# A decoder block's last stage rebuilt: its weights loaded before the branch, split once and kept, and its projection taken one token tile at a time

## The chip, the cores and the metric

The kernel runs on one core of a Trainium2 chip. The metric is device time in microseconds (us) of one launch; lower is better.

## The reference

Two networks run one after the other on 256 tokens of width 1024, all in float32. The change touches the end of the second one:

```python
x = x + _hier_moe(_rmsnorm(x, norm_ffn_g[i]), ...)          # 32 experts, top 2
hp = _rmsnorm(x, norm_ple_g[i])
x = x + (p[i] @ w_ple[i]) * jax.nn.sigmoid(hp @ w_ple_gate[i])
return _rmsnorm(x, final_norm_g)
```

`w_ple` is 256 x 1024 and multiplies a per-token embedding p; `w_ple_gate` is 1024 x 1024. In the mixture of experts each expert has `w_gate_e`, `w_up_e` (1024 x 256) and `w_down_e` (256 x 1024).

## The kernel before

The program is written out by hand, engine by engine: the functions `tensor` (PE), `scalar` (ACT), `vector` (DVE), `gpsimd` and `sync` (SP) each issue their instructions in a fixed order and wait on semaphores. Nothing reorders them later.

**Weights.** SP issues every weight transfer on one queue, in the order of the list `units` (about 1 MB each). A unit goes to a slot of `ring` (7 slots of 8 KB per partition) or, in the mixture stage, of `ringx` (5 more). Before it issues a unit, SP waits until the unit that held that slot is used up. The stage of the experts is a stream: expert pair i (experts 2i and 2i+1) has four units of gate/up weights, each filled by two transfers (`w_gate_e`, `w_up_e`), and two units of down weights. Units 0 to 3 of the last pair, 15, sit in ring slots 0 to 3. The embedding weight follows in slot 6, which held a unit of pair 14, and the four units of the gate weight follow in slots 0 to 3: the first two wait for the first halves of `gate_up(15)`, the last two for its second halves (the semaphores `gate_up_used` and the bank's `full`).

**Splits.** Where precision asks for it, a float32 weight is split into a high part (an ACT copy to fp32r, `wh`) and the rest (a DVE subtraction, `wl`), in chunks of 128 x 1024: `split_hi` and `split_lo` with room for three chunks (`c % 3`), so a chunk waits until PE has used the one three before it. Each gate unit is two chunks. A product then takes three matmuls: high by high, high by low, low by high.

**Experts.** For each pair i PE does `gate_up(i)` (64-column weight tiles, 128 x 512), ACT the Silu into `fs`, DVE the product `fa`, PE two transposes (`act_T(i)`), ACT the copy `rt2` (`at2`, out of PSUM), PE `scatter(i - 1)` and `down(i)`, ACT and DVE the split halves `ysh` and `ysl` of the scaled result. `scatter(15)` closes the sum in banks 0 to 3, and DVE adds it to x (`add_x`).

**The branch.** If an expert has more than 64 tokens, a slow path computes the excess. Every engine but GpSimd reaches `general(...)`: it waits for the last `add_x`, loads a flag into a register and jumps over the path's body if the flag is 0, as it is here. On PE the body is some 450 rows long. SP issues the embedding and gate weights only behind its own branch.

**The end.** PE multiplies the embedding by `w_ple` (16 float32 matmuls) into banks 0 to 3. ACT squares x, DVE and ACT make the reciprocal root, both scale x into `xs` (`norm_T("np2")`), PE transposes it, ACT writes `hh` and DVE `hl`. `gemm_tok` then does the gate's projection: for each half of the columns, four chunks, both token tiles (96 matmuls). ACT takes the sigmoid, DVE multiplies and adds into x, and a last norm over both tiles (`norm_x`) goes out in two transfers of 512 KB.

Of the kernel before, what the change touches and what calls it, by code (L numbers as in the profile page):

```python
# [6 lines left out]
ALU = mybir.AluOpType  # L7
# [5 lines left out]
P = 128  # L13
# [78 lines left out]
def build(nc, A, out):  # L92
    with ExitStack() as ctx:
# [50 lines left out]
        def opened(*shapes):  # L144
# [41 lines left out]
        r1, S_, xg, ScT, ysh, ysl, xh, xl, smr, wsl, ringx = opened(  # L186
            ("S_", [P, 2, 2, 512], F32R), ("xg", [P, 2, 8, S], F32), ("ScT", [P, 4, S], F32R),
            ("ysh", [P, 2, DM], F32R), ("ysl", [P, 2, DM], F32R), ("xh", [P, 2, DM], F32R), ("xl", [P, 2, DM], F32R),
# [3 lines left out]
        r1, whp, wlp, sg, hhp, hlp = opened(*W2, ("sg", [P, 2, 1024], F32), *HH)  # L192
# [76 lines left out]
        c_gate = [split_of(cols_of(A["w_ple_gate_2"][0], n * 512, 512), 1024) for n in range(2)]  # L269
# [171 lines left out]
        flag = scr[:, 650:651].bitcast(I32)  # L441
# [6 lines left out]
        RV = {n: i + 1 for i, n in enumerate(("an0", "ckn", "fn0", "an1", "fn1", "mid", "nm2", "cq", "mln", "nf2", "np2", "fin"))}  # L448
        tnorm = {n: i for i, n in enumerate(("an0", "fn0", "an1", "fn1", "nm2", "nf2", "np2"))}
        SQ = {"an0": 4, "fn0": 8, "an1": 12, "fn1": 16, "mid": 17, "nm2": 21, "nf2": 25, "np2": 29, "fin": 30}  # L450
# [3 lines left out]
        def tensor(e):  # L454
# [585 lines left out]
            def scatter(i):  # L1040
                emptied(q, "ScT", i // 2)
                for n in range(2):
                    emptied(q, "dn", i, n)
                    for t in range(2):
                        b = claim(2 * t + n, "moe", t, n) if i == 0 else bank[2 * t + n]
                        for v in (ysh, ysl):
                            w = mm(b[:, :], ScT[:, i % 4, t * P:(t + 1) * P], v[:, i % 2, n * 512:(n + 1) * 512],
                                   i == 0 and v is ysh, i == 15 and v is ysl)
                        if i == 15:
                            w.then_inc(of(full, "moe", t, n), 1)  # L1050
                if i < 15:
                    ysc.inc(w, i)
# [30 lines left out]
            for n in range(2):  # L1083
                gemm_tok(("gate", n), "np2", c_gate[n], 512, hhp, hlp, whp, wlp, (4 + 2 * n, 5 + 2 * n))

        def scalar(e):
# [28 lines left out]
            def norm_T(name, ready, hh, c0=None, h2=None):  # L1115
# [14 lines left out]
                for i in range(4):  # L1130
                    if c0 is None and i % 2 == 0:
                        continue
                    b = filled(q, name, i)
                    for j in range(2):
                        k = 2 * i + j
                        w = act(hh[:, k, :], b[:, j * S:(j + 1) * S], ACT.Copy, scale=gain(name, k))
                        if c0 is not None:
# [285 lines left out]

            for part in range(2):
                gather(0, part)
            for i in range(16):
# [13 lines left out]
                for n in range(2):  # L1440
# [15 lines left out]
            act(xs[:, 0, :], x[:, 0, :], ACT.Square, accum_out=st[:, 0:1]).then_inc(s_sq, 1)  # L1456
            q.wait_ge(s_var, RV["fin"])
            act(st[:, 16:18], st[:, 8:10], ACT.Sqrt).then_inc(s_std, 1)

        def vector(e):  # L1460
# [48 lines left out]
            def rinv(name, n, width, o):  # L1509

                ts(st[:, 8:8 + n], st[:, 0:n], 1.0 / width, EPS, ALU.mult, ALU.add).then_inc(s_var, 1)
                q.wait_ge(s_std, RV[name])
                rcp(o, st[:, 16:16 + n]).then_inc(s_rstd, 1)
                q.wait_ge(s_rstd, RV[name])

            def norm_T(name, hh, hl=None, c0=None, h2=None, l2=None):
# [6 lines left out]
                if hl is not None:  # L1523
# [590 lines left out]

            select(0)
            for part in range(2):
                gather(0, part)
            for i in range(16):
# [13 lines left out]
                for n in range(2):  # L2132
# [4 lines left out]
                        ALU.subtract).then_inc(of(drained, "dn", i, n), 1)  # L2137
            add_x("moe")
# [3 lines left out]
            norm_T("np2", hhp, hlp, c_gate[0], whp, wlp)  # L2142
            for n in range(2):
                for c in range(4):
                    split_lo(min(c_gate[n] + c + 3, len(chunks)), whp, wlp)
                for t in range(2):
                    g_, o = sg[:, t, n * 512:(n + 1) * 512], x[:, t, n * 512:(n + 1) * 512]
                    emptied(q, ("gate", n), t)
# [4 lines left out]
            norm_x("fin", 1, xs, lambda: q.wait_ge(s_sgm, 4))  # L2153
# [16 lines left out]
        def sync(e):  # L2170
# [17 lines left out]
            for t in range(2):  # L2188
                q.wait_ge(s_xn, 3 + t)
                e.dma_start(od[:, t, :], xs[:, t, :]).then_inc(s_out, 16)  # L2190
            e.wait_ge(s_out, 32)
# [4 lines left out]
        wb = [ring[:, i, :] for i in range(3)]  # L2196
# [115 lines left out]
```

## Time and profile before

| | us |
|---|---|
| three runs | 1272.15, 1272.04, 1267.53; median 1272.04 |
| the profiled execution, its own time | 1272.39 |
| its span in the profile | 1270.6 |
| PE busy | 1126.4 (89%) |
| DVE busy | 625.7 (49%) |
| ACT busy | 498.8 (39%) |
| DMA, mean over the span | 177 GB/s |

The span runs from the first to the last recorded instruction; the execution's own time is 1.8 us more, outside the records. All times of day below are us from the span's start. The experts' stream fills the stretch from about 965 to 1216, and the part that the change rebuilds is the last 55 us.

### The profile page before, as it was taken

What the parts mean: (1) busy time and instruction counts of PE and PEld (TensorE: products, weight loads), DVE (VectorE), ACT (ScalarE), POOL (GpSimd) and SP (SyncE); (2) the same over time, 40 slices, a digit from 0 to 9 for tenths busy, and PEclk for the clock granted to TensorE, in tenths of its full rate; (3) what the DMA queues carried; (4) which work ended last, traced back from release to release, by engine and by line L of the source; (5) the groups of instructions that cost most, each with busy time, mean ns of one, the idle gap of its engine ahead of it and who ended that gap; (6) DMA issues with size and microseconds to landing.
All of it is one profiled execution on the core that took longest, in us unless ns stands there. A gap on an engine that the chain in (4) does not pass through costs nothing.

```text
span 1270.6 us, 15565 instructions
## 1 busy us (share of the span) xinstructions
PE 1126.4 (89%) x6207; PEld 883.4 (70%) x6207; DVE 625.7 (49%) x1222; ACT 498.8 (39%) x868; POOL 11.6 (1%) x10
## 2 busy tenths in 40 slices
PE   6777999899999899798999997978658999999866
PEld 5665768899988776687999986857545445554335
DVE  4677324666664554545676645656652112211135
ACT  5433212655553544335555535364231112121143
POOL 0000000000000000000000000000020000000000
PEclk9895657899999999779999998977878999999988
DMA  9520004456555443214565552320077999999940
GB/s 353 192 96 1 1 1 152 133 179 192 175 198 192 140 166 100 67 41 149 176 189 176 200 178 84 126 70 1 1 261 278 377 378 380 381 379 379 345 168 33
DMA packets 157502, 225.13 MB, mean 177 GB/s; under 512 B 9319, under 2 KB 124402, under 8 KB 157426
## 3 DMA queue, kind: packets, MB, share of 16 engines
q1 hardware_dynamic: 155168, 221.04, 51.3%
q10 hardware_dynamic: 2258, 3.05, 0.7%
q8 instruction: 51, 0.84, 0.3%
q14 instruction: 25, 0.20, 0.0%
HBM read 223.02 MB, written 1.05 MB: 176 GB/s over the span
## 4 chain that ended last, share of the span: by engine, by line
PE 80%; DVE 10%; ACT 4%; DMA 3%; issue 2%; SPq 1%; ACTq 1%; DVEq 0%
PE ps L472 73%; PE ps L476 6%; ACT xs L1091 1%; DVE wl L1467 1%; DMA pos<-in_positions_dram 1%; ACT wh L1094 1%; SPq L2186 1%; DMA ring<-in_w_up_e_dram 1%; DVE smb L1481 1%; DVE smb L1467 1%; DVE x L1467 1%; ACTq L1180 1%; DVE big L1733 0%; DVE xs L1467 0%; DVE sA L1477 0%
## 5 line engine op out<-in xcount | busy, mean ns | idle before, releaser
L1467 DVE TENSOR_TENSOR wl<-ring,wh 128x1024 fp32r<-128x1024 f32 (+2 forms) x220 | 267.8, 1220 | 242.5 <-ACT wh L1094 241.9
L1094 ACT ACTIVATE wh<-ring 128x1024 fp32r<-128x1024 f32 (+2 forms) x220 | 231.6, 1055 | 281.0 <-PE ps L472 275.1
L472 PE MATMUL ps<-hh,wh 128*128 128x256 f32 x768 | 219.9, 286 | 1.7 <-ACT sA L1094 0.9
L472 PE MATMUL ps<-hl,wh 128*128 128x256 f32 x768 | 218.2, 284 | 0.0
L472 PE MATMUL ps<-hh,wl 128*128 128x256 f32 x768 | 218.1, 284 | 0.0
L472 PEld LDWEIGHTS ps<-hh,wh 128*128 128x128 f32 x768 | 148.3, 193 | 3.2 <-issue 2.0
L472 PEld LDWEIGHTS ps<-hl,wh 128*128 128x128 f32 x768 | 148.2, 193 | 0.6 <-issue 0.5
L472 PEld LDWEIGHTS ps<-hh,wl 128*128 128x128 f32 x768 | 148.2, 193 | 0.0
L472 PE MATMUL ps<-wh,hh 128*128 128x512 f32 (+2 forms) x224 | 92.4, 412 | 6.0 <-DVE big L1485 2.7
L472 PE MATMUL ps<-ring,xg 128*64 128x512 f32 (+1 forms) x352 | 90.6, 565 | 1.9 <-DMA ring<-in_w_up_e_dram 1.9
L472 PE MATMUL ps<-wl,hh 128*128 128x512 f32 (+2 forms) x224 | 89.7, 400 | 0.0
L472 PE MATMUL ps<-wh,hl 128*128 128x512 f32 (+2 forms) x224 | 89.6, 400 | 0.0
L1091 ACT ACTIVATE pb<-smb,nbb 128x128 f32<-128x128 f32 x80 | 35.7, 447 | 97.6 <-DVE nbb L1472 97.6
L472 PEld LDWEIGHTS ps<-ring,xg 128*64 128x64 f32 (+1 forms) x352 | 31.5, 143 | 57.0 <-issue 52.9
L1477 DVE SCALAR_TENSOR_TENSOR ysl<-ps,wsl,ysh 128x512 fp32r<-128x512 f32 x32 | 24.0, 751 | 91.9 <-ACT ysh L1091 91.9
L476 PE MATMUL ps<-cst,xs 128*128 128x128 f32 x160 | 33.0, 392 | 39.0 <-ACT xs L1091 30.4
L476 PEld LDWEIGHTS ps<-cst,xs 128*128 128x128 f32 x160 | 30.1, 211 | 41.9 <-ACT xs L1091 32.6
L472 PE MATMUL ps<-ringx,xg 128*64 128x512 f32 x192 | 57.4, 593 | 1.0 <-DMA ringx<-in_w_up_e_dram 1.0
L1467 DVE TENSOR_TENSOR fa<-ps,fs 128x256 f32<-128x256 f32 x16 | 6.8, 425 | 101.0 <-ACT fs L1091 101.0
L472 PEld LDWEIGHTS ps<-wh,hh 128*128 128x128 f32 x224 | 44.2, 197 | 17.2 <-issue 7.9
L472 PE MATMUL ps<-wl,ffh 128*128 128x512 f32 x176 | 54.3, 389 | 0.0
L472 PE MATMUL ps<-wh,ffh 128*128 128x512 f32 x176 | 54.2, 390 | 0.0
(237 smaller groups left out, 1718.8 us busy)
## 6 DMA issues: line engine op xcount, KB each, us to landing
ring<-in_w_up_dram SPq DMA_DIRECT2D x88, 512.0 KB, 4.8
ring<-in_w_down_dram SPq DMA_DIRECT2D x22, 1024.0 KB, 4.9
ring<-in_w_gate_e_dram SPq DMA_DIRECT2D x40, 512.0 KB, 10.3
ring<-in_w_up_e_dram SPq DMA_DIRECT2D x40, 512.0 KB, 9.2
ringx<-in_w_down_e_dram SPq DMA_DIRECT2D x16, 1024.0 KB, 9.6
ring<-in_w_down_e_dram SPq DMA_DIRECT2D x16, 1024.0 KB, 10.7
ring<-in_w_in_odd_dram SPq DMA_DIRECT2D x12, 1024.0 KB, 5.1
ringx<-in_w_gate_e_dram SPq DMA_DIRECT2D x24, 512.0 KB, 8.3
```

Of the source, the lines that this page charges most:

```text
L472: return e.matmul(o, l, r, start=start, stop=stop)
L476: return e.transpose(o, i, cst[0:n, C_ID:C_ID + n])
L1091: return e.activation(o, i, f, **kw)
L1094: return e.activation(o, i, ACT.Copy)
L1180: e.dma_start(dst, src).then_inc(s_c, 16)
L1467: return e.tensor_tensor(o, a, b, op)
L1477: return e.scalar_tensor_tensor(out=o, in0=a, scalar=s, in1=b, op0=o1, op1=o2)
L1481: return e.tensor_tensor_reduce(out=o, in0=a, in1=b, scale=1.0, scalar=init, op0=o1, op1=o2, accum_out=ac)
L2186: e.dma_start(view(slot[k]), src).then_inc(loaded[k], 16)
```

## The change

- SP issues the embedding and gate weights before its branch, right behind the last expert's; the slow path now uses `ringx` for its weights, and its flag moves to a tile that nothing overwrites.
- All eight split chunks of the gate weight have room of their own, `wg` (64 KB per partition, over tiles of the expert stage). The first three are split in the expert loop, at the end of iteration i = 14; the other five after the norm.
- The gate's projection takes token tile 0 over all eight chunks, then tile 1. The sigmoid, product, sum, final norm and stores of tile 0 come before those of tile 1; squares are on ACT alone, in halves, and stores are four of 256 KB.
- `scatter` goes through the banks by token tile, and ACT has `warm()` (a square root of a constant) before the branch and before the last squares.

```diff
@@ tiles @@
-        r1, S_, xg, ScT, ysh, ysl, xh, xl, smr, wsl, ringx = opened(
+        r1, S_, xh, xl, xg, ScT, ysh, ysl, smr, wsl, ringx = opened(
...
-        r1, whp, wlp, sg, hhp, hlp = opened(*W2, ("sg", [P, 2, 1024], F32), *HH)
+        r1, wg, hhp, hlp, sg = opened(("wg", [P, 8, 2, 1024], F32R), *HH, ("sg", [P, 2, 1024], F32))
@@ tensor: scatter @@
-                for n in range(2):
+                for t, n in ((0, 0), (0, 1), (1, 0), (1, 1)):
                     emptied(q, "dn", i, n)
-                    for t in range(2):
@@ tensor, end @@
             norm_T("np2")
-            for n in range(2):
-                gemm_tok(("gate", n), "np2", c_gate[n], 512, hhp, hlp, whp, wlp, (4 + 2 * n, 5 + 2 * n))
+            for t in range(2):
+                tk = slice(t * P, (t + 1) * P)
+                for c in range(8):
+                    n = c // 4
+                    q.wait_ge(w_split, c_gate + c + 1)
+                    emptied(q, "np2", c % 4)
+                    for k in (2 * (c % 4), 2 * (c % 4) + 1):
+                        b = claim(4 + 2 * t + n, "gate", t, n) if k == 0 else bank[4 + 2 * t + n]
+                        wh_, wl_ = (wg[:, c, i, (k % 2) * 512:(k % 2 + 1) * 512] for i in range(2))
+                        mm(b[:, :], hhp[:, k, tk], wh_, k == 0, False)
+                        mm(b[:, :], hhp[:, k, tk], wl_, False, False)
+                        w = mm(b[:, :], hlp[:, k, tk], wh_, False, k == 7)
@@ scalar @@
+            def gate_hi(upto):
+                while hi[0] < c_gate + upto:
+                    c = hi[0]
+                    u, half, n, _ = chunks[c]
+                    copy(wg[:, c - c_gate, 0, :], unit_in(q, u)[:, half * n:(half + 1) * n]).then_inc(w_hi, 1)
+                    hi[0] += 1
...
                     act(ysh[:, i % 2, n * 512:(n + 1) * 512], b[:, :], ACT.Copy, scale=wsl[:, i:i + 1]).then_inc(s_yh, 1)
+                if i == 14:
+                    filled(q, "wsl", 7)
+                    gate_hi(3)
+            warm()
             general(e, "ACT")
...
-            norm_T("np2", added("moe"), hhp, c_gate[0], whp)
-            for n in range(2):
-                for c in range(4):
-                    split_hi(min(c_gate[n] + c + 3, len(chunks)), whp)
-                for t in range(2):
-                    b = filled(q, ("gate", n), t)
-                    act(sg[:, t, n * 512:(n + 1) * 512], b[:, :], ACT.Sigmoid).then_inc(of(drained, ("gate", n), t), 1)
-            q.wait_ge(s_sgm, 3)
-            act(xs[:, 0, :], x[:, 0, :], ACT.Square, accum_out=st[:, 0:1]).then_inc(s_sq, 1)
-            q.wait_ge(s_var, RV["fin"])
-            act(st[:, 16:18], st[:, 8:10], ACT.Sqrt).then_inc(s_std, 1)
+            norm_T("np2", added("moe"), hhp, hl_too=True)
+            gate_hi(8)
+            for t in range(2):
+                for n in range(2):
+                    b = filled(q, "gate", t, n)
+                    act(sg[:, t, n * 512:(n + 1) * 512], b[:, :], ACT.Sigmoid).then_inc(of(drained, "gate", t, n), 1)
+                if t:
+                    warm()
+                for n in range(2):
+                    c = slice(n * 512, (n + 1) * 512)
+                    q.wait_ge(s_sgm, 2 * t + n + 1)
+                    act(xs[:, t, c], x[:, t, c], ACT.Square, accum_out=st[:, 2 * n + t:2 * n + t + 1]).then_inc(s_sq, 1)
+                q.wait_ge(s_var, RV[f"fin{t}"])
+                act(st[:, 16 + t:17 + t], st[:, 8 + t:9 + t], ACT.Sqrt).then_inc(s_std, 1)
@@ vector: gate_lo as gate_hi, subtracting into wg[:, c - c_gate, 1, :] @@
+                if i == 14:
+                    gate_lo(3)
             add_x("moe")
             general(e, "DVE")
...
+            norm_T("np2", hhp, hlp)
+            gate_lo(8)
...
+                q.wait_ge(s_sq, SQ[f"fin{t}"])
+                own.inc(tt(st[:, t:t + 1], st[:, t:t + 1], st[:, 2 + t:3 + t], ALU.add))
+                rinv(f"fin{t}", 1, DM, st[:, 24 + t:25 + t], t)
+                for n in range(2):
+                    c = slice(n * 512, (n + 1) * 512)
+                    stt(xs[:, t, c], x[:, t, c], st[:, 24 + t:25 + t], gfin[:, 1, c], ALU.mult, ALU.mult).then_inc(s_xn, 1)
@@ sync @@
             for u, (_, parts) in enumerate(units):
-                if u == u_ple:
-                    general(e, "SP")
...
+            general(e, "SP")
...
-            for t in range(2):
-                q.wait_ge(s_xn, 3 + t)
-                e.dma_start(od[:, t, :], xs[:, t, :]).then_inc(s_out, 16)
+            for i in range(4):
+                t, c = i // 2, slice((i % 2) * 512, (i % 2 + 1) * 512)
+                q.wait_ge(s_xn, 3 + i)
+                e.dma_start(od[:, t, c], xs[:, t, c]).then_inc(s_out, 16)
```

How this moves instructions stands in the built programs. On SP, the issues around the branch (TENSOR_LOAD begins it). Before:

```order
L2186 DMA ring<-in_w_down_e_2_dram 128x2x1024 [waits full7]
L2186 DMA ring<-in_w_down_e_2_dram 128x2x1024
L2202 TENSOR_LOAD smb_14 [waits drained3,flag_ready]
...
L2186 DMA ring<-in_w_ple_2_dram 128x2x1024 [waits gate_up_used]
L2186 DMA ring<-in_w_ple_gate_2_dram 128x4x512 [waits gate_up_used] x3
L2186 DMA ring<-in_w_ple_gate_2_dram 128x4x512 [waits full6]
```

With the change:

```order
L2225 DMA ring<-in_w_down_e_2_dram 128x2x1024 [waits full7]
L2225 DMA ring<-in_w_down_e_2_dram 128x2x1024
L2225 DMA ring<-in_w_ple_2_dram 128x2x1024 [waits gate_up_used]
L2225 DMA ring<-in_w_ple_gate_2_dram 128x4x512 [waits gate_up_used] x3
L2225 DMA ring<-in_w_ple_gate_2_dram 128x4x512 [waits full6]
L2243 TENSOR_LOAD st [waits drained3,flag_ready]
```

The five transfers now stand ahead of the branch, with the same waits.

On ACT, from the last `ysh` of iteration 14 to the first of iteration 15 (`fs<-ps6` is the Silu of `gate_up(15)`; `loaded0` and `loaded1` count the landings in ring slots 0 and 1). Before:

```order
L1091 ACTIVATE ysh_14<-ps4,wsl_14 128x512 [waits y_scattered,full4,drained6]
L1091 ACTIVATE ysh_14<-ps5,wsl_14 128x512 [waits full5]
L1091 ACTIVATE fs<-ps6 128x256 [waits full6]
L1094 ACTIVATE rt2<-ps7 128x256 [waits full7]
L1091 ACTIVATE ysh_14<-ps4,wsl_14 128x512 [waits y_scattered,full4]
```

With the change:

```order
L1103 ACTIVATE ysh_14<-ps5,wsl_14 128x512 [waits full5]
L1106 ACTIVATE wg_15<-ring 128x1024 [waits loaded0]
L1106 ACTIVATE wg_15<-ring 128x1024
L1106 ACTIVATE wg_15<-ring 128x1024 [waits loaded1]
L1103 ACTIVATE fs<-ps6 128x256 [waits full6]
L1106 ACTIVATE rt2<-ps7 128x256 [waits full7]
```

Three copies of gate chunks, with waits for the first two gate units, stand ahead of the Silu; on DVE three subtractions stand ahead of `fa` in the same way.

## Rows read from the trace of the kernel before

**Rows 1.** The chain of waits, from 1191 us on: start, length, what it was.
```profile
1191.86 9.34 DMA ring<-in_w_up_e_dram
...
1201.25 3.66 PE ps L472 x14
...
1205.42 0.43 DVE fa L1467
...
1214.18 1.89 DVE x L1467 x3
...
1217.44 5.61 DMA ring<-in_w_ple_dram
...
1223.09 9.41 PE ps L472 x16
...
1236.51 23.01 PE ps L472 x93
```
**Rows 2.** Timeline of SP: its last weight issues (start, length, engine, line, operation).
```profile
1193.22 2.63 SPq L2186 DMA_DIRECT2D ring<-in_w_down_e_dram  x2
1217.44 0.37 SPq L2186 DMA_DIRECT2D ring<-in_w_ple_dram  x1
1217.86 4.15 SPq L2186 DMA_DIRECT2D ring<-in_w_ple_gate_dram  x4
```
**Rows 3.** Stretches: length, busy us by engine, granted PE clock, DMA share, GB/s.
```profile
532.00:558.00 26.00, 26.00 (x104) 21.74 (x105) 9.22 (x37) 8.71 (x33) 0.00 (x0) 0.50 0.00 1
...
1203.00:1206.00 3.00, 2.00 (x9) 0.53 (x6) 0.42 (x1) 0.38 (x1) 0.00 (x0) 1.00 0.30 123
...
1217.50:1223.10 5.60, 0.01 (x1) 0.01 (x1) 1.38 (x5) 5.27 (x12) 0.00 (x0) 0.50 0.83 287
1223.10:1227.50 4.40, 4.40 (x5) 1.83 (x6) 0.36 (x1) 1.06 (x1) 0.00 (x0) 0.50 1.05 393
1227.70:1232.50 4.80, 4.80 (x14) 2.12 (x13) 0.67 (x1) 0.00 (x0) 0.00 (x0) 1.00 1.03 378
1238.10:1241.00 2.90, 2.90 (x8) 2.26 (x7) 1.32 (x2) 0.16 (x1) 0.00 (x0) 0.50 0.00 0
```
**Rows 4.** Timeline of PE: its last matmul before the branch.
```profile
1214.22 0.40 PE L472 MATMUL ps<-ysl,ScT 128*128 128x512 f32 x1
```
**Rows 5.** The branch's line (L2202) by engine: durations in ns, first and last start.
```profile
L2202 ACTq COMPARE_BRANCH  x1: 50/50/50, 1216.9 to 1216.9; - x1
L2202 PEldq COMPARE_BRANCH  x1: 3862/3862/3862, 1217.1 to 1217.1; - x1
```
**Rows 6.** Timeline of ACT and DVE behind the branch.
```profile
1217.39 0.63 ACT L1091 ACTIVATE xs<-x 128x512 f32<-128x512 f32 x1 [4.88 <-issue]
...
1219.96 1.28 ACT L1091 ACT_TABLE_LOAD   x1
1221.26 0.20 ACT L1091 ACTIVATE st<-st 128x2 f32<-128x2 f32 x1
1221.70 1.33 ACT L1091 ACTIVATE xs<-x,st 128x512 f32<-128x512 f32 x2 [0.23 <-DVE st L1493]
1226.05 1.06 ACT L1094 ACTIVATE wh<-ring 128x1024 fp32r<-128x1024 f32 x1 [3.02 <-DMA ring<-in_w_ple_gate_dram]
1227.14 1.23 DVE L1467 TENSOR_TENSOR wl<-ring,wh 128x1024 fp32r<-128x1024 f32 x1 [4.56 <-ACT wh L1094]
```
**Rows 7.** Timeline of the end.
```profile
1259.80 0.39 PE L472 MATMUL ps<-wh,hl 128*128 128x512 f32 x1
1261.51 0.68 DVE L1467 TENSOR_TENSOR sg<-sg,ps 128x512 f32<-128x512 f32 x1
1262.23 0.69 DVE L1467 TENSOR_TENSOR x<-x,sg 128x512 f32<-128x512 f32 x1
1264.29 0.17 DVE L1473 TENSOR_SCALAR st<-st 128x2 f32<-128x2 f32 x1
1264.93 2.48 DVE L1477 SCALAR_TENSOR_TENSOR xs<-x,st,gfin 128x1024 f32<-128x1024 f32 x2
```

More of the change, by code:

```diff
@@ L268, in build @@
                              A["w_ple_2"][0].rearrange("(k p) n -> p k n", p=P)))
-        c_gate = [split_of(cols_of(A["w_ple_gate_2"][0], n * 512, 512), 1024) for n in range(2)]
+        c_gate = [split_of(cols_of(A["w_ple_gate_2"][0], n * 512, 512), 1024) for n in range(2)][0]
         place, in_slot, landed = {}, [None] * (NU + NX), [0] * (NU + NX)
@@ L440, in build @@
         tot = scr[:, 616:648]
-        flag = scr[:, 650:651].bitcast(I32)
+        flag = st[:, 63:64].bitcast(I32)
         def slots_of(i, t):
@@ L1041, in scatter @@
                 emptied(q, "ScT", i // 2)
-                for n in range(2):
+                for t, n in ((0, 0), (0, 1), (1, 0), (1, 1)):
                     emptied(q, "dn", i, n)
-                    for t in range(2):
[L1045 to L1050, printed above, removed]
+                    b = claim(2 * t + n, "moe", t, n) if i == 0 else bank[2 * t + n]
+                    for v in (ysh, ysl):
+                        w = mm(b[:, :], ScT[:, i % 4, t * P:(t + 1) * P], v[:, i % 2, n * 512:(n + 1) * 512],
+                               i == 0 and v is ysh, i == 15 and v is ysl)
+                    if i == 15:
+                        w.then_inc(of(full, "moe", t, n), 1)
                 if i < 15:
@@ L1082, in tensor @@
             norm_T("np2")
-            for n in range(2):
-                gemm_tok(("gate", n), "np2", c_gate[n], 512, hhp, hlp, whp, wlp, (4 + 2 * n, 5 + 2 * n))
+            for t in range(2):
[10 more added lines that the diff above has]
+                        w = mm(b[:, :], hlp[:, k, tk], wh_, False, k == 7)
+                    if k == 7:
+                        w.then_inc(of(full, "gate", t, n), 1)
         def scalar(e):
@@ L1113, in warm, with norm_T @@
                 act(st[:, 62:63], cst[:, C_ONE:C_ONE + 1], ACT.Sqrt)
-            def norm_T(name, ready, hh, c0=None, h2=None):
+            def norm_T(name, ready, hh, c0=None, h2=None, hl_too=False):
                 for t in range(2):
@@ L1130, in norm_T @@
                 for i in range(4):
-                    if c0 is None and i % 2 == 0:
+                    if c0 is None and not hl_too and i % 2 == 0:
                         continue
@@ L1136, in norm_T @@
                         w = act(hh[:, k, :], b[:, j * S:(j + 1) * S], ACT.Copy, scale=gain(name, k))
-                        if c0 is not None:
+                        if c0 is not None or hl_too:
                             w.then_inc(s_hh, 1)
@@ L1522, in norm_T @@
                     ts(xs[:, 1, c], x[:, 1, c], st[:, 25:26], None, ALU.mult).then_inc(s_xsd, 1)
-                if hl is not None:
+                if c0 is not None:
                     split_lo(c0 + 1, h2, l2)
@@ L2113, in gather, with gate_lo @@
                 cp(xg[:, g % 2, 2 * m:2 * m + 2, :].rearrange("p k c -> p (k c)"), b[:, :]).then_inc(of(drained, "xg", g, m), 1)
+            def gate_lo(upto):
+                while lo[0] < c_gate + upto:
+                    c = lo[0]
+                    u, half, n, _ = chunks[c]
+                    q.wait_ge(w_hi, c + 1)
+                    tt(wg[:, c - c_gate, 1, :], slot[place[u][0]][:, half * n:(half + 1) * n],
+                       wg[:, c - c_gate, 0, :].bitcast(F32), ALU.subtract).then_inc(w_split, 1)
+                    lo[0] += 1
             select(0)
@@ L2137, in vector @@
                         ALU.subtract).then_inc(of(drained, "dn", i, n), 1)
+                if i == 14:
+                    gate_lo(3)
             add_x("moe")
             general(e, "DVE")
[L2142 to L2145, printed above, removed]
-                for t in range(2):
+            norm_T("np2", hhp, hlp)
+            gate_lo(8)
+            for t in range(2):
+                for n in range(2):
                     g_, o = sg[:, t, n * 512:(n + 1) * 512], x[:, t, n * 512:(n + 1) * 512]
-                    emptied(q, ("gate", n), t)
+                    emptied(q, "gate", t, n)
                     b = filled(q, "ple", t, n)
```

21 lines of the change are left out of this document (10 added, 11 removed).

## The prediction

> **What bounds the kernel now.** I read the chain of waits first, for the path that sets the end. Through the experts it is the weight stream: PE waits for the last expert's weights until 1201.25 [rows 1]. From there it is one dependent chain: the second half of `gate_up(15)`, ended 1204.9; Silu and `fa` at 1205.42; PE to the last matmul of `scatter(15)`, ended 1214.6 [rows 4]; `add_x`, ended 1216.07 [rows 1]; the branch; the landing of the embedding weight, from 1217.44 to 1223.05; sixteen embedding matmuls, 9.41 us; transposes and `hh`/`hl`; the gate's 96 matmuls from 1236.51 to 1260.2 [rows 1, 7]; and a tail of 10.4 us to the end of the span at 1270.6.
>
> The timeline of SP shows that its queue stands idle from 1195.85 (1193.22 + 2.63) to 1217.44 [rows 2]: the change wants this hole. The stretches show why the hole in the queue is no hole in the transfers: the engines move at full rate until 1203 and only drain from 1203 to 1206 [rows 3]. They show the clock of TensorE too: at 1.00 (2.4 GHz) while the experts run, and at 0.50 (1.2 GHz) from 1217.5, some 3 us after PE fell idle, until 1227.5, that is for 4.4 us after it had work again.
>
> **The change part by part.** *The early split.* On ACT three copies of gate chunks now stand ahead of the Silu of pair 15, and the third waits for the second gate unit. When does that land? The stream from 1203 to 1206 moved 3 x 123 GB/s = 0.37 MB; at 378 to 393 GB/s [rows 3] that is 1.0 us, so evenly spread it would have ended at 1204.0, and its slowest engine ended near 1206. Behind it come the embedding unit and two gate units, 3.15 MB or 8.1 us. None is issued too late to follow on: the first two gate units wait only for the first halves of `gate_up(15)`, over before PE's wait for the last expert's weights, which ends at 1201.25 [rows 1]. So the landing lies between 1212.1 (even) and 1214.1 (the slowest engine's); a unit has landed only when its slowest engine has, so I take 1213.6, near the upper end. The first two copies are over by then. Then 1.06 us for the third copy and 1.23 for its subtraction [rows 6], with gaps: `fa` starts at 1216.0 where it started at 1205.42. **+10.6 us.** Queued behind the waiting instructions are the Silu, `rt2` and both `ysh` on ACT, `fa`, both `ysl` and `add_x` on DVE; and PE, which cannot transpose before `fa`, nor run `scatter(14)`, which stands behind the transposes.
>
> *The clock in the rest of pair 15.* PE now idles from 1204.9 to about 1216.5, longer than the 8.5 us ahead of 1223.09 [rows 1], after which the clock stayed low for 4.4 us [rows 3]. Taken the same, 4.4 us at half speed lose **2.2 us**. Bounds: 1.4 us from the shortest low stretch shown, 2.9 us; 5.7 us if the clock stays low as in the 26 us from 532 [rows 3]. `add_x` then ends at 1216.07 + 12.8 = 1228.9.
>
> *The wait for the embedding weight* is gone: it has landed by about 1208. What is late next? ACT restarted 1.32 us after `add_x` (1217.39), but PE's jump over the slow path took 3.86 us, from 1217.1 to 1221.0, against 0.05 on ACT [rows 5, 6]. It was hidden under the transfer; now it is bare. PE can start 4.9 us after `add_x`, not 7.0: **-2.1 us**. That is all that the early load brings at this place. PE will start at 1233.8 after 6.4 us of idling, so I keep the sixteen matmuls at 9.41 us, with 4.4 us of low clock; with no low stretch they would take 7.2 (bound: -2.2). Running sum +10.7 where the transposes start: 1243.2.
>
> *The norm beside it.* The square root of `warm()` makes one table load more, ahead of the squares: 1.28 us [rows 6]. ACT's path from its restart to the scaled x was 5.6 us (1217.39 to 1223.03), now 6.9: from 1230.2 to 1237.1, 6.1 us before PE is free. Nothing, as long as PE's restart stays late; without that cover the norm would set the start of the transposes from 1237.1 on.
>
> *The splits kept, and the gate by token tile.* The matmuls are the same 96. A chunk now lasts PE six matmuls (1.36 us at 23.01/93 less the low stretch, about 0.227 each) instead of twelve; ACT makes one in 1.06 and DVE in 1.23, and three are ready, so PE does not wait. Bank 5 is no longer needed at the second matmul group, a wait of 0.2 us: **-0.2**. The low stretch of 2.9 us at 1238.1 [rows 3] I leave as it is; without it, -1.4. `scatter` by token tile: `add_x` takes the banks in the new order anyway, and its 1.89 us for three [rows 1] are DVE's own: 0.
>
> *The tail*, from the end of the last matmul: 10.4 us before. Now: sigmoid 0.60; then on ACT table load and root of `warm()`, 1.5, beside product and sum on DVE, 1.4 (0.68 + 0.69 [rows 7]); two squares, 1.4 with the read of the sum; four small steps, 0.7 with gaps 0.9; two halves of the product with the gain, 1.25 (half of 2.48 [rows 7]); and the store, 3.2 us before for 512 KB, between 2.5 and 3.2 for 256 KB, taken as 2.85. Sum 8.5, with 0.1 of gaps 8.6: **-1.8 us**. Tile 0's part lies beside tile 1's matmuls, 10.9 us. The table load here took 1.28 us and the root started 0.02 us behind it (1219.96, 1221.26 [rows 6]).
> The Trainium skill (ScalarE: Activation LUTs, What ACT_TABLE_LOAD costs) adds a drain and puts each switch at about 2.66 us. By that rule the tail would be 1.4 us longer and the estimated sum +10.1; the row shows no drain, and it decides.
>
> **Sum:** 10.6 + 2.2 - 2.1 - 0.2 - 1.8 = **+8.7 us**. The profiled execution took 1272.39, 0.35 above the median of 1272.04; against the median this gives **1280.7 us**. About 0.5% (6.4 us) is what a measurement of this kernel can tell from no change, so the bounds are 1265.7 and 1278.4.
>
> **The rivals.**
> *A, the loads come in time.* If the gate units landed before the Silu is due at 1204.93, the terms +10.6 and +2.2 go, and -4.1 is left: 1267.9. For it: SP is free from 1195.85, and the order of two transfers on sixteen engines is not shown by any row. Against: 3.15 MB more would have to move by 1204.9 on engines that were full until 1203. It decides if the third copy starts before about 1206. This is the case on the other side; it stays a small gain because of PE's jump, and only with a shorter store and a warm clock as well would it pass 1265.7.
> *B, PE's jump is short.* Its 3.86 us coincided with SP's issue of five transfers, which will be absent. If it was these that held it up, PE restarts with ACT, 1.3 us after `add_x`: -3.6, and after a shorter idle about -1.0 for the clock: 1276.1. Against: ACT, DVE and SP jumped at the same moment in under 0.1 us, and the transfers moved 287 GB/s on average from 1217.5 to 1223.1 [rows 3], 1.6 MB, so at full rate they ran only from about 1219.
> The Trainium skill (Runtime: NRT & Kernel Launch, Instruction fetch mechanics) says that a taken branch whose target lies outside the window of prefetched pages must fetch it by DMA before the engine goes on. By this the 3.86 us belong to PE's long slow path and stay; it is why B gets no more than it does, and the trace agrees as far as one jump can.
> *C, the clock stays low* from the restart at 1216.5 through the embedding matmuls. For it: two long gaps close together, and 26 us of low clock with PE busy from 532 on [rows 3]. Against: after the one gap shown here PE had the clock back in 4.4 us. Price: 5.7 + 0.7 for the last scatter instead of 2.2, and 13.6 for 9.4 us: +8.4, 1289.
>
> **How the numbers follow.** The forecast has 0.71, A 0.12, B 0.12, C 0.05. The forecast's own range: downward the landing 1.5, the clock 0.8 + 2.2 + 1.4, the store 0.35; upward the landing 0.5, the store 0.35, a longer low clock 1.5, a drain 1.4. Not all fall together: 1276 to 1284. The range that holds 8 in 10 takes in B and the edges on both sides, and leaves out A and C: 1269 to 1286. Of the forecast's 0.71, 0.58 lie above 1278.4. Slower: 0.58 + 0.05 = 0.63. Within 0.5%: 0.13 + 0.12 (B) + 0.08 (A) = 0.33. Faster: 0.04, the rest of A.
>
> **What the profile would show.** If I am right: the third copy into `wg` starts near 1213.6 behind a wait for `ring<-in_w_ple_gate_dram`; `fa` of pair 15 at about 1216; PE idle for over 10 us before it and the clock at 0.50 behind it; PE's COMPARE_BRANCH again near 3.9 us, and embedding matmuls that wait for nothing but it, from about 1234; the gate's matmuls without waits for `wg`; 8 to 9 us from the last matmul to the end. I am wrong if the Silu starts before 1210, if PE's jump takes under 1 us, or if the clock is back within 1 us of the restart.

## The result and the profile after

| | us |
|---|---|
| with the change, four runs | 1279.93, 1280.49, 1280.09, 1281.36; median 1280.29 |
| before, four runs (the three shown and 1267.32) | median 1269.78 |
| ratio | 1.008, 95% interval 1.0055 to 1.0104 |
| the profiled execution: own time, span | 1279.93, 1278.1 |

The change makes the kernel 0.8% slower. The two kernels' profiled executions lie 7.5 us apart (1279.93 for 1272.39), the medians 10.5: two of the kernel before's four runs are near 1267.4 and two near 1272.1, while all four of the change are near 1280 (the end of the section on the prediction says what hangs on that).

The chain of waits of the changed kernel, from 1188 us on (start, length, what it was), answers to [rows 1]:

```profile
1188.43 9.41 PE ps L473 x40
...
1197.86 15.95 DMA ring<-in_w_ple_gate_dram
...
1213.83 1.07 ACT wg L1106
...
1214.91 0.30 DVE wg L1493
...
1216.06 0.43 DVE fa L1493
1216.48 0.04 issue
1216.53 0.69 PE ps L477 x2
...
1226.47 1.89 DVE x L1493 x3
1228.36 4.98 issue
1233.34 9.03 PE ps L473 x16
...
1246.38 23.66 PE ps L473 x96
```

The chain no longer leads through the experts' last weights: for 16 us it is the transfer of the gate weight, then the third early copy and its subtraction, then `fa`. Behind the last sum stand 4.98 us in which PE waits for nothing that the profile shows. 3.82 of them are PE's jump; the rest is mostly the load of the flag ahead of it. The branch's line and SP's timeline, answering to [rows 5] and [rows 2]:

```profile
L2243 ACTq COMPARE_BRANCH  x1: 50/50/50, 1229.2 to 1229.2; - x1
...
L2243 PEldq COMPARE_BRANCH  x1: 3822/3822/3822, 1229.4 to 1229.4; - x1
```
```profile
1195.19 0.66 SPq L2225 DMA_DIRECT2D ring<-in_w_ple_dram  x1
1197.33 10.04 SPq L2225 DMA_DIRECT2D ring<-in_w_ple_gate_dram  x4
```

The timeline of ACT shows the wait and, at the end, the tail:

```profile
1213.83 1.06 ACT L1106 ACTIVATE wg<-ring 128x1024 fp32r<-128x1024 f32 x1 [0.71 <-DMA ring<-in_w_ple_gate_dram]
1214.79 0.37 ACT L1103 ACTIVATE fs<-ps 128x256 f32<-128x256 f32 x1
...
1270.06 0.60 ACT L1103 ACTIVATE sg<-ps 128x512 f32<-128x512 f32 x1 [4.65 <-PE ps L473]
1270.68 1.28 ACT L1103 ACT_TABLE_LOAD   x1
1271.97 0.20 ACT L1103 ACTIVATE st<-cst 128x1 f32<-128x1 f32 x1
```

And the stretches (columns as in [rows 3]: length, busy us by engine, granted clock of PE, DMA share, GB/s):

```profile
1203.00:1206.00 3.00, 1.39 (x6) 0.21 (x2) 0.00 (x0) 0.00 (x0) 0.00 (x0) 1.00 1.02 403
1207.00:1216.50 9.50, 0.00 (x0) 0.00 (x0) 3.92 (x4) 3.33 (x4) 0.00 (x0) 0.50 1.01 373
1216.50:1220.10 3.60, 3.57 (x10) 2.80 (x10) 0.00 (x0) 0.38 (x1) 0.00 (x0) 0.50 0.12 46
1220.30:1223.90 3.60, 3.60 (x17) 1.05 (x16) 0.73 (x1) 0.69 (x1) 0.00 (x0) 1.00 0.00 0
```

From 1203 to 1206 the engines moved 403 GB/s instead of 123: the stream does not drain, it goes on. PE idles at half clock (1.2 GHz) and has 3.6 us of work before the clock is back at 2.4 GHz.

**Where the time went.** All kernels below are compared in one stretch, from the end of `gate_up(15)` (1204.90 before, 1204.39 with the change) to the end of the span. What lies ahead of it is the same code in all of them but for the order of the banks in `scatter`, yet the end of `gate_up(15)` varies by up to 11 us from one profiled execution to the next (last section). Each number is the start of the named instruction in the timeline less the end of `gate_up(15)`; the last two are ends.

| kernel | fa | end of last sum | embedding product | transposes | gate | last matmul | end of span |
|---|---|---|---|---|---|---|---|
| before | 0.52 | 11.16 | 18.19 | 27.44 | 31.61 | 55.29 | 65.70 |
| the change | 11.67 | 23.96 | 28.95 | 37.82 | 41.99 | 65.64 | 73.71 |
| e1_split_late | 0.52 | 11.16 | 16.23 | 26.07 | 30.25 | 52.25 | 60.33 |
| e2_loads_only | 0.52 | 11.18 | 15.92 | 24.50 | 28.67 | 52.32 | 62.76 |
| e3_short_body | 0.52 | 11.17 | 12.74 | 21.18 | 26.08 | 49.67 | 57.78 |
| e4_one_chunk | 8.99 | 21.02 | 25.79 | 34.62 | 38.79 | 62.51 | 70.65 |
| e5_wait_inside | 0.53 | 11.17 | 15.38 | 24.32 | 28.49 | 52.12 | 60.26 |
| e6_transposes_first | 0.52 | 11.17 | 19.77 | 16.04 | 26.23 | 48.60 | 56.75 |
| e7_filler | 11.68 | 22.32 | 26.85 | 36.81 | 40.98 | 63.03 | 71.16 |
| e8_all | 0.52 | 11.16 | 19.45 | 15.93 | 25.92 | 48.29 | 55.81 |
| e9_before_short | 0.53 | 11.17 | 18.62 | 27.61 | 31.78 | 55.48 | 65.87 |
| e10_late_pair | 0.52 | 11.16 | 12.92 | 22.86 | 27.04 | 49.06 | 57.14 |
| e11_product_around | 0.52 | 11.17 | 12.91 | 17.86 | 24.67 | 46.73 | 54.32 |

The runs' times agree with this table once that variation is taken out. Each run has a granted clock, its mean over the span, and the runs of one kernel fall into groups by it. The group with the lowest clock (0.898 to 0.904), less the same group of the kernel before in the same session (0.899 to 0.900):

| kernel | runs in the group, median | against the kernel before | in the stretch |
|---|---|---|---|
| e1_split_late | 6, 1267.4 | -4.7 | -5.4 |
| e2_loads_only | 8, 1269.4 | -2.6 | -2.9 |
| e3_short_body | 9, 1264.8 | -7.2 | -7.9 |
| e4_one_chunk | 8, 1277.0 | +4.9 | +4.95 |
| e5_wait_inside | 7, 1266.5 | -5.5 | -5.4 |
| e6_transposes_first | 3, 1263.6 | -8.5 | -8.95 |
| e7_filler | 3, 1277.3 | +5.3 | +5.5 |
| e8_all | 7, 1262.5 | -9.6 | -9.9 |
| e9_before_short | 6, 1272.0 | +0.2 | +0.2 |
| e11_product_around | 3, 1261.3 | -10.5 | -11.4 |

### The profile page after: what moved, and what is told of

Read it like the earlier page. It is cut to its first block, busy times and chain, and to the rows that moved or that the text cites. A ratio compares the mean times of both kernels' runs of the same rounds, so it can differ in the third digit from the quotient of the medians.

```text
span 1278.1 us, 15581 instructions
## 1 busy us (share of the span) xinstructions
PE 1127.0 (88%) x6207; PEld 884.0 (69%) x6207; DVE 625.7 (49%) x1226; ACT 506.0 (40%) x881; POOL 11.6 (1%) x10
## 4 chain that ended last, share of the span: by engine, by line
PE 79%; DVE 10%; ACT 4%; DMA 3%; issue 2%; SPq 1%; ACTq 1%; DVEq 0%
PE ps L473 73%; PE ps L477 6%; ACT xs L1103 2%; DVE wl L1493 1%; DMA ring<-in_w_ple_gate_dram 1%; DMA pos<-in_positions_dram 1%; ACT wh L1106 1%; DVE smb L1507 1%; DVE smb L1493 1%; SPq L2225 1%; DMA ringx<-in_w_up_e_dram 1%; ACTq L1192 1%; DVE x L1493 1%; DVE xs L1493 0%; DVE big L1759 0%
## 5 line engine op out<-in xcount | busy, mean ns | idle before, releaser
L1493 DVE TENSOR_TENSOR wl<-ring,wh 128x1024 fp32r<-128x1024 f32 (+2 forms) x212 | 258.3, 1220 | 231.2 <-ACT wh L1106 230.5
L1106 ACT ACTIVATE wh<-ring 128x1024 fp32r<-128x1024 f32 (+2 forms) x212 | 223.3, 1055 | 269.2 <-PE ps L473 266.2
L473 PE MATMUL ps<-wh,hh 128*128 128x512 f32 (+2 forms) x192 | 78.9, 411 | 3.8 <-DVE big L1511 2.7
L473 PE MATMUL ps<-wl,hh 128*128 128x512 f32 (+2 forms) x192 | 76.3, 397 | 0.0
L473 PE MATMUL ps<-wh,hl 128*128 128x512 f32 (+2 forms) x192 | 75.9, 395 | 0.0
L473 PE MATMUL ps<-wh,ffl 128*128 128x512 f32 x176 | 54.2, 389 | 0.0
```

What stands on the lines that cost most here:

```text
L473: return e.matmul(o, l, r, start=start, stop=stop)
L1106: return e.activation(o, i, ACT.Copy)
L1493: return e.tensor_tensor(o, a, b, op)
```

## The experiments

The theory going in: the wait for the second gate unit and the clock it lets fall cost 12.8 us, and PE's jump eats most of what the early load could give back.

**e1_split_late: the early split undone.**

```diff
-                if i == 14:
-                    filled(q, "wsl", 7)
-                    gate_hi(3)
...
-            norm_T("np2", added("moe"), hhp, hl_too=True)
+            norm_T("np2", added("moe"), hhp, hl_too=True, mid=lambda: gate_hi(3))   # behind the scaling of xs
```
(and the same on DVE with `gate_lo`)

> The changed kernel with one part undone: no gate chunk is split inside the expert loop; the first three are split on ACT and DVE behind the norm's scaling, while PE does the embedding product. Theory (the third copy waits for the second gate unit and holds up the Silu of pair 15, which also lets PE's clock fall): both terms go, 10.6 + 2.2, so about 12.5 us under the changed kernel and 4.1 us under the kernel before; the Silu of pair 15 within 0.5 us of its place in the kernel before, the embedding product about 2 us earlier than there because it starts when PE's jump ends. Rival (the loss comes from the transfers themselves or from the new tail, and the split's place is innocent): the time stays within 2 us of the changed kernel.

Measured: 1264.15 us median against 1271.45 for the kernel before on the same chip, ratio 0.9957 (0.9934 to 0.998); some 16 us under the change, of which 3 are the higher clock of half of its runs (its six at 0.900 to 0.902 have a median of 1267.4, 12.9 under the change). In the stretch 13.4 us under the change, 5.4 under the kernel before. The Silu of pair 15 starts 0.04 us behind `gate_up(15)`, as before. So nearly all the loss hangs on where three copies stand, and not on the transfers or the new tail. The 1.3 us beyond the forecast 4.1 are no gain of the edit alone: the gate's matmuls took 22.0 us and not 23.65, since the low stretch in them was absent, while the product took 10.01 for 9.41; the tail gave 0.5 more than forecast.

**e2_loads_only: the early loads alone, in the kernel before.**

```diff
-                if u == u_ple:
-                    general(e, "SP")
...
+            general(e, "SP")
             od = out[0].rearrange("(t p) d -> p t d", p=P)
...
-        wb = [ring[:, i, :] for i in range(3)]
+        wb = [ringx[:, i, :] for i in range(3)]
```

> The kernel before with one part of the change alone: SP issues the embedding and gate weights ahead of its branch. Theory (PE's jump over the slow path takes 3.9 us and stood hidden under the transfer): 2.1 us faster than the kernel before, the embedding product starts at the end of PE's COMPARE_BRANCH, 4.9 us after the last sum. Rival 1 (the jump was held up by SP's issues at the same moment): PE restarts about 1.3 us after the sum and the gain is 5.7 us or more. Rival 2 (the extra transfers behind the experts' delay the last expert weights): no gain, and PE waits past 1201.3 for the last expert's weights.

Measured: 1269.0 median, ratio 0.9991 (0.9968 to 1.0014); by all its runs it cannot be told from the kernel before. The stretch shows what happened, 2.9 us less, and the runs of like clock show 2.6. In its chain of waits there is a hole of 4.7 us where the transfer of 5.61 us stood:

```profile
1213.84 1.89 DVE x L1467 x3
1215.73 4.73 issue
1220.46 8.74 PE ps L472 x16
```

The product starts 2.27 us earlier (15.92 for 18.19) and is 0.67 shorter (8.74 for 9.41). Rival 1 is out; so is rival 2, for the last expert's weights come no later: the wait for them ends at 1200.89 here, 1201.25 before.

**e3_short_body: PE has little to jump over.**

```diff
-            for n in range(32):
+            for n in range(1):
```
(in the four bodies of the slow path, on top of e1_split_late; `g_dve` is waited for accordingly)

> The first experiment's kernel with the slow path cut to expert 0 (it leaves out the excess of the other 31 experts; that path is jumped over here). Theory (the target of PE's jump lies far behind the body, and its instructions have to be fetched): PE's COMPARE_BRANCH falls from 3.9 us to under 0.2, PE restarts about 1.3 us after the sum, and the kernel gains 2 to 4 us over the first experiment, less than 3.6 where the norm on ACT then sets the start of the transposes. Rival (a fixed price of a jump on PE, or the flag's load): the jump keeps 3.8 us and the time is the first experiment's.

The branch's line on PE, in e1_split_late and then here:

```profile
L2242 PEldq COMPARE_BRANCH  x1: 3885/3885/3885, 1208.5 to 1208.5; - x1
```
```profile
L2242 PEldq COMPARE_BRANCH  x1: 365/365/365, 1217.6 to 1217.6; - x1
```

The price of the jump goes with the length of what is jumped over: 3.89 us over 32 experts' rows, 0.37 over one's (these two lengths alone were tried). The trace shows what it is. DMA queue 8 carries packets of 16 KB of the kind "instruction". In the eleven kernels with the long body such a packet lies inside PE's jump, and the jump ends 1.3 to 1.4 us after the packet has landed: 1209.99 to 1210.95 in e1_split_late, whose jump ends at 1212.34. In the two with the short body none does; the next begins 0.75 us behind the jump. So PE waits for a fetch of instructions.

The restart comes 3.5 us earlier, the end of the stretch only 2.55. The product was 1.4 us shorter than in e1_split_late (8.61 for 10.01); against that the transposes to the gate took 0.7 more (4.90 for 4.18), because ACT still had the three copies ahead of `hh`, and the gate's matmuls 1.6 more, their low stretch being back. The medians show none of it: 1264.68 against 1264.15, ratios 0.9958 and 0.9957. But only one of the ten runs here has a clock above 0.902, against six of twelve in e1_split_late; the groups of lowest clock lie 2.6 us apart (1264.8 and 1267.4), as the stretch does. The expected gain of 2 to 4 us held.

**e4_one_chunk: a shorter wait.**

```diff
-                    gate_hi(3)
+                    gate_hi(1)
...
-                    gate_lo(3)
+                    gate_lo(1)
```

> The changed kernel with one chunk split early in place of three, so that the Silu of pair 15 waits for the first gate unit alone. Theory (the stall ends at a landing): the copy starts near 1211.1 as in the changed kernel, the Silu near 1212.1, DVE's product fa near 1213.4 instead of 1216.06; about 2.6 us faster than the changed kernel, still some 5.5 us slower than the kernel before. Rival (the stall is the time of the copies and subtractions on ACT and DVE): two of three pairs of 1.0 and 1.2 us go, and the product starts 2.2 us after the ysl of pair 14, near 1198, before its data is there, so that the whole loss vanishes.

```profile
1211.61 1.06 ACT L1106 ACTIVATE wg<-ring 128x1024 fp32r<-128x1024 f32 x1 [16.39 <-DMA ring<-in_w_ple_gate_dram]
1212.58 0.37 ACT L1103 ACTIVATE fs<-ps 128x256 f32<-128x256 f32 x1
```

Measured: 1276.73 median, ratio 1.0049 (1.003 to 1.0067). `fa` starts 2.7 us sooner than with three chunks, by the distance between the two landings, and 4.95 of the 8.0 us of loss stay. One copy of 1.06 us holds up the Silu by 7.7. The rival (the work of splitting) is out.

**e7_filler: the idle without the clock's fall.**

```diff
                 b = take("aT", i)
+                if i == 15:
+                    for _ in range(12):
+                        mm(b[:, :], cst[:, C_ID:C_ID + P], cst[:, C_MA:C_MA + 512], True, True)
                 emptied(q, "gu", i)
```

> The changed kernel with twelve float32 matmuls of constants on PE, some 10 us, into the bank that the transposes of pair 15 overwrite, issued while PE waits for fa; nothing of the result depends on them. Theory (the idle of 12 us costs the clock besides the wait itself): fa stays near 11.7 us behind the end of gate_up(15), the clock stays at 1.00 through scatter(14), its matmuls are 0.23 us apart and not 0.43, and from fa to the last sum it takes 10.6 us as in the kernel before instead of 12.3, so about 1.7 us less in the stretch to the end. The clock after PE's jump can come out either way, worth up to 2 us. Rival (scatter(14) and down(15) are slow for another reason, such as transfers or port traffic): 12.3 us and 0.43 us stay.

Its stretches around `fa`, which starts at 1207.32 there:

```profile
1196.00:1207.00 11.00, 10.13 (x24) 4.18 (x22) 3.19 (x3) 3.34 (x4) 0.00 (x0) 1.00 1.04 387
1207.40:1211.00 3.60, 3.21 (x16) 2.01 (x18) 0.33 (x1) 0.38 (x1) 0.00 (x0) 1.00 0.21 79
```

With PE kept busy through the wait its clock stays at 2.4 GHz, and from `fa` to the last sum it takes 10.64 us, exactly as in the kernel before, against 12.29 with the change. The clock's share of the loss is 1.65 us. The whole stretch is 2.55 us shorter than with the change: besides the 1.65, PE's jump is 0.46 shorter (3.36 for 3.82) and the gate's matmuls, without a low stretch here too, 1.6 (22.05 for 23.65), while the product takes 1.1 longer (10.12 for 9.03). Median 1272.9, ratio 1.0043 (1.0013 to 1.0072).

**e9_before_short: the jump in the kernel before.** The edit of e3_short_body, on the kernel before.

> The kernel before with the slow path cut to expert 0 (it leaves out the excess of the other 31; the path is jumped over). Theory (in the kernel before PE's jump is hidden under the embedding weight's transfer): COMPARE_BRANCH falls from 3.9 us to some 0.4, the embedding product still starts at the landing, 18.2 us behind gate_up(15), and the time stays within 0.3%. Rival (the jump cost the kernel before something too): the product starts earlier and the stretch to the end falls by over 1 us.

Measured: 1271.54 against 1271.27, ratio 1.0 (0.9978 to 1.0022), with COMPARE_BRANCH at 0.36 us and the product at 18.62. The jump cost the kernel before nothing; it was under the transfer.

**e5_wait_inside: jump earlier.**

```diff
             b, n = use["moe", 1, 1]
-            e.wait_ge(drained[b], n + 1)
             with e.If(e.value_load(flag[0:1, :], min_val=0, max_val=1) > 0):
+                e.wait_ge(drained[b], n + 1)
```
(on top of e1_split_late)

> The first experiment's kernel; the wait for the last sum stands inside the slow path instead of ahead of its test, so that all engines jump as soon as they reach it. Theory (PE's jump of some 3.7 us is bare): PE jumps right behind scatter(15), 1.4 us earlier, and the embedding product starts 14.8 us behind gate_up(15) instead of 16.2; 1.4 us faster than the first experiment, 59 us from gate_up(15) to the end. Rival (the norm on ACT, with its added table load, sets the transposes): the embedding product starts earlier but the transposes do not, and nothing is gained.

Measured: 1266.24, ratio 0.9958 (0.9934 to 0.9982), no better than e1_split_late; the stretch 0.07 us shorter. The transposes start 1.75 us earlier, but the gate's matmuls take 1.6 more (23.63 for 22.00), their low stretch being back. The product starts 0.85 us earlier, not 1.4. The jump begins 2.8 us earlier and takes 5.7 us:

```profile
L2241 PEldq COMPARE_BRANCH  x1: 5745/5745/5745, 1214.5 to 1214.5; - x1
```
```profile
1214.50:1216.00 1.50, 0.83 (x4) 0.34 (x2) 1.50 (x3) 1.49 (x2) 0.00 (x0) 1.00 1.04 384
1216.00:1218.00 2.00, 0.00 (x0) 0.00 (x0) 0.32 (x1) 2.00 (x8) 0.00 (x0) 0.93 0.73 268
```

The second fence has the stretches in which it lies: the gate weights were still streaming. The instruction packet begins 3.3 us behind the start of the jump (1217.82 for 1214.54), against 1.0 to 1.5 in the kernels that jump behind the sum, and the jump ends 1.4 us after it, as there. So it is the start of the fetch that is late. This was a miss, and gave the next question.

**e10_late_pair: no stream beside the jump.**

```diff
+                if u >= u_ple + 3:
+                    emptied(q, "moe", 1, 1)
                 for view, src in parts:
                     e.dma_start(view(slot[k]), src).then_inc(loaded[k], 16)
```
(on SP, on top of e5_wait_inside)

> The kernel with the wait inside the slow path (PE's jump there took 5.7 us and not 3.8), with the last two gate units issued only behind the last sum, so that no weight transfer runs while PE's jump begins. Theory (the jump has to fetch instructions over the same DMA engines, and the weight stream, at full share until 1216 there, delayed that fetch): PE's COMPARE_BRANCH falls from 5.7 to some 3.7 us, the embedding product starts 13.2 to 13.7 us behind gate_up(15) instead of 15.4. Rival (the jump waits for something of PE's own, such as the matmuls still running when it is reached): 5.7 us stay.

```profile
L2243 PEldq COMPARE_BRANCH  x1: 3367/3367/3367, 1215.6 to 1215.6; - x1
```
```profile
1215.60:1217.00 1.40, 0.81 (x4) 0.35 (x2) 1.40 (x3) 1.39 (x2) 0.00 (x0) 1.00 0.04 12
```

With 12 GB/s beside it instead of 384 the same jump takes 3.37 us, although PE's own matmuls still run when it begins, as in e5_wait_inside. The product starts 12.92 us behind `gate_up(15)`, even before the 13.2 expected. The instruction packet begins 1.0 us behind the start of the jump. The rival is out. This kernel was run once (1265.22 us); its profile is what is read.

**e6_transposes_first** moves `norm_T("np2")` on PE ahead of the embedding product (on top of e5_wait_inside) and splits all eight chunks behind `hh` and `hl`.

> The kernel with the wait inside, and on PE the transposes of the scaled x ahead of the embedding product, so that ACT and DVE make hh, hl and the first split chunks under it; all eight chunks are split behind hh and hl. Theory: the 4.2 us from the transposes to the first gate matmul leave the path; the transposes start when the norm is ready, which the table load behind the jump sets, near 17 us behind gate_up(15), the gate at 28 to 29, and the stretch ends near 57. Rival (the splits of the first chunks now come too late, since hl ends first): PE waits for w_split between the product and the gate, and less than 2 us is gained.

Measured: 1258.69, ratio 0.9911 (0.9873 to 0.9949). `hh`, `hl` and the first splits now lie under the product, and the gate starts 2.3 us earlier than in e5_wait_inside. The transposes started at 16.0, not 17, and the gate at 26.2, not 28 to 29.

**e8_all** moves `warm()` from ahead of the branch to behind it, and squares the first half ahead of the last sigmoid.

> The previous kernel with warm() behind the branch instead of ahead of it, which takes the extra table load off the norm's path, and with the square of the first half ahead of the last sigmoid. Theory: the transposes start when PE's jump ends, near 14.8 us behind gate_up(15) instead of 17, the gate near 26, and the tail is 0.6 us shorter than 8.1; 54 to 55 us from gate_up(15) to the end against 65.7 in the kernel before, about 0.9% faster than it. Rival (PE's clock, low after the idle of the jump, takes the gain back in the transposes and the embedding product): above 57 us.

Measured: 1262.25, ratio 0.9939 (0.9912 to 0.9966). The tail is 7.52 us instead of 8.15, as expected. The gain at the transposes did not come (15.93 against 16.04). Two things end late and nearly together, and I had reckoned with neither. PE's jump takes 5.7 us (6.0 in e6_transposes_first) and ends at 1215.08. The norm is later still, and it is what the transposes wait for:

```profile
1214.31 0.16 DVE L1491 TENSOR_TENSOR st<-st 128x2 f32<-128x2 f32 x1 [3.16 <-issue]
```
```profile
1215.92 3.39 PE L477 MATMUL ps<-cst,xs 128*128 128x128 f32 x14 [5.76 <-ACT xs L1103]
```

ACT's last square was done at 1212.07, yet DVE's first step of the norm began at 1214.31, 3.1 us behind DVE's own COMPARE_BRANCH of 0.07 us. The same hole of 2.8 to 3.2 us stands there in all five kernels in which the squares are done early (e5, e6, e8, e10, e11). So DVE seems to pay for its jump as well, behind the branch's row and not in it; a run that shortens DVE's path alone was not made, so this is not shown. 55.8 us for the stretch against 54 to 55 expected.

**e11_product_around** puts the two findings together.

```diff
             for t in range(2):
+                if t:
+                    norm_T("np2")
                 for n in range(2):
                     b = claim(2 * t + n, "ple", t, n)
```
(on top of e8_all, with the edit of e10_late_pair)

> The kernel with all changes so far, with the last two gate units issued behind the last sum as in e10_late_pair, and with the embedding product of token tile 0 ahead of the transposes and that of tile 1 behind them, since PE is then free before the norm is ready. Theory: the product starts near 13.4 us behind gate_up(15), the transposes at 17 to 18, the gate at 23 to 24 instead of 25.9; 53 to 54 us to the end instead of 55.8, about 1% under the kernel before. Rival (the transfers issued behind the sum land too late for the fifth chunk, or PE's low clock stretches the first half of the product): the gate starts at 25 us or later, or PE waits inside it.

Measured: 1258.38 us median against 1271.27, ratio 0.9908 (0.9884 to 0.9932): 0.9% faster than the kernel before and 1.7% under the change (1258.38 to 1280.29, medians of two sessions). It has the shortest stretch, 54.32 us against 65.70 and 73.71. The gate started at 24.67, not 23 to 24; the timeline of PE shows it waiting 0.65 us for the first split at the end:

```profile
1212.69 5.11 PE L473 MATMUL ps<-ring,ppT 128*128 128x512 f32 x8 [2.73 <-issue]
...
1220.20 3.60 PE L473 MATMUL ps<-ring,ppT 128*128 128x512 f32 x8
1224.45 0.73 PE L473 MATMUL ps<-wg,hh 128*128 128x512 f32 x2 [0.65 <-DVE wg L1492]
```

By time e6_transposes_first is as good; the stretch tells them apart (56.75 and 54.32), the runs do not.

## Why the prediction was right

| step | forecast | measured in the stretch |
|---|---|---|
| `fa` waits for the second gate unit | +10.6 | +11.15 (11.67 for 0.52) |
| low clock behind the wait | +2.2 | +1.65 (12.29 for 10.64 from `fa` to the end of the last sum) |
| wait for the embedding weight gone, PE's jump bare | -2.1 | -2.04 (4.99 for 7.03) |
| embedding product | 0 | -0.38 (9.03 us for 9.41) |
| start of the transposes to the gate | 0 | 0.00 (4.17 both) |
| gate's 96 matmuls | -0.2 | -0.03 |
| tail | -1.8 | -2.34 (8.07 for 10.41) |
| sum | +8.7 | +8.0 |

The steps are differences of the table's rows, the lengths of the product from the two chains of waits.

- **The landing.** Forecast at 1213.6 between 1212.1 and 1214.1; the copy started at 1213.83. Behind the end of `gate_up(15)`, which came 0.5 us earlier than before, that is 9.44 us and not 8.7, just past the upper bound of 9.2. The end of the slowest engine was the better of the two guesses; which engine ended last was not read. e4_one_chunk shows that the landing sets the stall.
- **The clock.** The mechanism is shown by e7_filler. 2.2 was too high: PE worked at the low clock for only 3.6 us, until 1220.1, not 4.4.
- **The jump.** That the early load would give only 2.1 us was the least obvious step. e2_loads_only bears it out, and e3_short_body with its instruction packets shows the cause. The Trainium skill (Runtime: NRT & Kernel Launch, Instruction fetch mechanics) says that a taken branch out of the prefetched pages stalls for a fetch by DMA; 3.89 us against 0.37 agree with it. Rival B was half right: transfers do lengthen the jump, but those of the kernel before came too late to do so (3.86 us with them, 3.82 without, the instruction packet 1.0 us behind the start of the jump in both). The prediction's "ACT, DVE and SP jumped at the same moment in under 0.1 us" reads the branch's rows alone: DVE's next instruction there starts 3.19 us behind its branch, some 0.4 us after the last square. With the change the squares end later (1233.51, and DVE goes on at 1233.54), so this cost nothing here.
- **The tail** was mis-sized by 0.5 us. From the last matmul to the start of the last two products with the gain it took 4.2 us (1270.04 to 1274.25), forecast 4.4 to 4.5; the rest is their length and the store of 256 KB.
- **The table load** is not dearer than its row: 1.28 us, and the root 0.01 us behind it. The Trainium skill's drain (ScalarE: Activation LUTs, What ACT_TABLE_LOAD costs) does not show here: the load follows the sigmoid by 0.02 us. The 1.4 us for a drain in the forecast's own range upward has thus no row of this kernel.
- **Rivals A and C** did not come. In A the third copy would have started before 1206. In C the clock would have stayed low; it was back after 3.6 us. (C's 13.6 us for the product at low clock should be 14.4, twice the 7.2 that the prediction has at full clock; its price is 0.8 too small, and nothing else rests on it.)

That the median came within 0.4 us of the forecast is partly luck. The sum was 0.7 us too high in the stretch. The median of the kernel before moved from 1272.04 to 1269.78 with one run more, and 8.7 on top of that would have been 1278.5. It helped that no run of the change fell into a group of higher clock: all four had 0.896 to 0.897. The forecast was reckoned from the kernel before's level near 1272, which in its later runs goes with the lowest clock (0.900, against 0.905 near 1267); against its two runs at that level the change costs 8.2 us, close to the 8.0 of the stretch.

## What to carry to other kernels

Work moved forward into a loop brings its waits along: ask what the engine has queued behind it, and when the data lands if its queue is a stream that is already full. Before a wait is taken off the path, look for what ran unseen under it; here it was a jump over a long unused path, worth 3.5 us at the restart and 2.6 at the end, and it was cheapest when little was jumped over and no stream ran beside it. Small differences are read in the stretch that was changed, from a common event, when the rest of the kernel varies by more; and runs are compared with runs of the same granted clock.

## What the runs showed of the hardware that I had not expected

**A jump shares the DMA engines.** The same jump on PE took 3.37 us with 12 GB/s of transfers beside it, 3.4 to 3.9 in the kernels that jump behind the sum, and 5.7 to 6.0 beside a stream of some 385 GB/s (e5, e6, e8). The instruction packet in it began 1.0 to 1.5 us behind the start of the jump without the stream and 3.2 to 3.5 with it; from its landing to the end of the jump it was 1.3 to 1.4 us in all eleven.

**The clock in the attention stage comes in more than one course.** In the profiled executions `gate_up(15)` ended between 1195.6 and 1206.3, with nearly the same code ahead of it. The stretch from 145 to 160 us, in the kernel before and in e1_split_late:

```profile
145.00:160.00 15.00, 14.39 (x41) 9.09 (x42) 4.21 (x22) 4.31 (x17) 0.00 (x0) 0.52 0.00 0
```
```profile
145.00:160.00 15.00, 13.69 (x69) 9.07 (x69) 6.18 (x29) 5.30 (x21) 0.00 (x0) 1.00 0.00 0
```

PE does 41 matmuls at half clock in the one and 69 at full clock in the other. Summed over the spans up to 1190, the clock was low for 235.5 us before and 218.5 in e1_split_late, where `gate_up(15)` ends 8.6 us sooner. Over the thirteen profiled executions this sum takes three values, and `gate_up(15)` ends with it: 235.5 us in nine (1204.2 to 1206.3), 221.9 in e8_all and e11_product_around (1200.0 and 1199.8), 218.5 in e1_split_late and e7_filler (1196.3 and 1195.6). That fits runs of one kernel that lie 10 us apart (e1_split_late: 1257.7 to 1268.33). What decides between them was not tried.

**The low stretch in the gate's matmuls** comes and goes too: 23.6 to 23.7 us for the 96 in seven of the kernels, 22.0 to 22.4 in the six others, with the same work. In three of the six (e1, e7, e10) the product ahead of it took 10.0 to 10.1 us, in the seven 8.6 to 9.4: part of what is saved in the gate was lost there. Differences of up to 1.6 us between two profiled executions can be this alone.
